# Seven-product stage: the second product ahead of the seventh, and the load of a and b ahead of that of the third block

## The chip, the cores and the metric

The kernel runs on one core of a Trainium2 chip. The metric is the device time of one execution in microseconds (us), lower being better. TensorE does the matrix products, ScalarE and VectorE split numbers and finish the activations, GpSimd and SyncE start transfers from the main memory (GpSimd also those that add to what is already in the on-chip buffer).

## The reference, cut to what matters

```python
# x: 512 tokens x 1024 features; one layer of three sub-layers
def _swiglu(h, w_in, w_out):
    g, u = jnp.split(h @ w_in, 2, axis=-1)      # h 512x1024, w_in 1024x5632
    return (jax.nn.silu(g) * u) @ w_out         # w_out 2816x1024
h = x * (1.0 + scale[:, 2, None, :]) + shift[:, 2, None, :]
y = _swiglu(h, ffn2_w_in[l], ffn2_w_out[l])     # the third sub-layer: here lies the change
x = _layernorm(ALPHA * x + 0.5 * gate[:, 2, None, :] * y, post_ln_g[l, 2], post_ln_b[l, 2])
```

Sub-layers before it are another such feed-forward layer and a mixer (attention and pooling). Everything is float32.

## The kernel before

Every float32 matrix product is made of three passes: each number is split into a rounded high part and the rest, and high times high, high times low and low times high are added up in PSUM. ScalarE makes the high parts (`ACT.Copy` into a rounded type), VectorE the rests (whole minus high), TensorE multiplies.

The first projection of the last feed-forward layer has 22 pairs of tiles: a gate tile and an up tile, each 128 output features by 1024 inputs, for 512 tokens. Pairs 0 to 4 are done plainly. Pairs `T0` = 5 to `FT - 1` = 21 are done by seven half-size products in place of eight, in the manner of Strassen and Winograd: the gate tile is cut into the blocks a and b, the up tile into c and d (each 128 x 512), the tokens into two halves of 256, and the products p1 to p7 use these blocks or their sums. "Block t" below is the work of one such pair. One product is four blocks of inputs by three passes, so 12 matmuls of 128x128 on 256 tokens.

The order of each engine is written out by hand, and semaphores tie them together:

- TensorE, `block_products` (line 1007): for each t p1, p5, p6 of block t, then p4 of block t-1, then p7 and p2 of block t, then p3 of block t-1. p1, p6 and p7 (and p4 later) are accumulated into the same bank, and ScalarE copies the bank's interim values out: `p1_copy` after p1, `u2` after p6, `u3` after p7. So p6 waits for the copy of p1, p7 for the copy `u2`, and p4 (a block later) for the copy `u3`. p2 goes to another bank, and waits for nothing but old sums.
- SyncE, the loop at line 847: in the iteration of t it issues `load_c(t + 2)` (256 KB, after p5 of t), `load_d(t)` (256 KB, after p4 of t-1), `load_a3(t + 2)` (256 KB, after p7 of t) and `load_ab(t + 2)` (512 KB, after p2 of t). A wait at its head holds what is behind it.
- GpSimd, `add_block`: when c of a block has landed, it issues a transfer that adds d to it (line 2574); when the third block (a, loaded by `load_a3`) has landed, one that adds c to it (line 2578). These two sums are the operands of p5 and p7, the tile `raw_13`.
- ScalarE, `block_stage` (line 1596), iteration t: round the two weight blocks of p4 and p3 of t-1 (`hi_d4`, line 1563), the second silu of t-2, copy p1 of t, the first silu of t-1, `a_high` of t-2, round a and b of t+1 (`hi_ab`, line 1540), copy `u2` of t (line 1578), round `raw_2` of t+1 (line 1547), round `raw_13` of t+1 (line 1555), copy `u3` of t (line 1583). The two in the middle matter here: the copy `u2` of a block stands behind the rounding of the next block's a and b.
- VectorE, `block_stage` (line 2204), iteration t: sums of t-2 and t-1, the rest of d4, the weight sums of t+1 (lines 2157 and 2161, which need a, b and the finished c+d), and the rests of ab, 2 and 13 of t+1 (line 2144), the last being the one that p5 of t+1 waits for.

`product_order` (line 93) lists the order of TensorE's products, and all waits on "product so-and-so of block t" are counts derived from that list. After the stage come the units of the second projection (`D2` and on); the first of them land in buffers that the seven products used, so their loads wait for products of the last two blocks.

Of the kernel before, what the change touches and what calls it, by code (L numbers as in the profile page):

```python
# [27 lines left out]
FT = D_FF // P  # L28
# [56 lines left out]
T0 = 5  # L85
D2 = F2 + 2 * T0
# [6 lines left out]
def product_order():  # L93

    out = []
    for t in range(T0, FT + 1):
        if t < FT:
            out += [("p1", t), ("p5", t), ("p6", t)]
        if t > T0:
            out.append(("p4", t - 1))  # L100
        if t < FT:
            out += [("p7", t), ("p2", t)]
        if t > T0:
            out.append(("p3", t - 1))
    return out
# [24 lines left out]
def sum_order():  # L130

    out = [("T", j) for j in range(4)] + [("s2", T0), ("s4", T0)]
    for t in range(T0, FT + 2):
        if t - 2 >= T0:
            out.append(("gb", t - 2))
        if T0 <= t - 1 < FT:
            out.append(("ga", t - 1))
        if t + 1 < FT:
            out += [("s2", t + 1), ("s4", t + 1)]
        if T0 <= t - 1 < FT:  # L140
            out += [("ub", t - 1), ("pa", t - 1)]
    return out
# [18 lines left out]
def counts(order, base):  # L161

    return {step: base + i + 1 for i, step in enumerate(order)}
# [90 lines left out]
def source(n, wunits):  # L254

    half = KD // 2 * P
    if S_FILL <= n < S_A:
        kind, first = FILL[2 * (n - S_FILL)][0], int(FILL[2 * (n - S_FILL)][1])
        if kind == "q":
            return wunits[U_UQ + first // 2]  # L260
        return wunits[U_OUT + first:U_OUT + first + 2, :, half:2 * half].rearrange("t p n -> p t n")
    if S_OUT <= n < F2:
        return wunits[U_OUT + SPLIT_TILES + n - S_OUT]
    if S_A <= n < S_OUT:
        first = 2 * (n - S_A)
        return wunits[U_OUT + first:U_OUT + first + 2, :, 0:half].rearrange("t p n -> p t n")
    return wunits[n if n < D2 else n - D2 + F2_DOWN][:, 0:unit_width(n)]
# [7 lines left out]
def unit_width(n):  # L275

    for down, end in ((F1_DOWN, MX), (D2, STREAM)):
        if down <= n < end and (n - down) % DPM == DPM - 1:
            return LAST_K * P
    return UNIT  # L280


def build(nc, xT, wunits, ada_w, c_rows, pos_rows, cols_dram, pool_w, outT):
# [4 lines left out]
    with ExitStack() as ctx:  # L288
# [84 lines left out]
        def raw_of(n, width):  # L373

            if n == D2:
                return raw_ab[1][:, 0:width]
            if n == D2 + 1:
                return raw_13[1][:, 0:width]
            return raw[:, n % RAWS, 0:width]
# [79 lines left out]
        def in_set(t):  # L459
            return (t - T0) % 2  # L460
# [6 lines left out]
        def raw13(t):  # L467
            return raw_13x if t == T0 + 1 else raw_13[in_set(t)]
# [57 lines left out]
        def pair_banks(t):  # L526
            return (bank[0], bank[1], bank[2]) if t % 2 == 0 else (bank[3], bank[6], bank[7])
# [119 lines left out]
        s_blk, s_bhi, s_blo, s_bsum = s_tp, s_fc, s_tok, s_xk  # L647
        PRODUCT = counts(product_order(), KD)
        ROUNDED = counts(rounding_order(), KD)
        REST = counts(rest_order(), 2 * QB)  # L650
        SUM = counts(sum_order(), QB)
# [68 lines left out]
        def _(sp):  # L720
# [7 lines left out]
            def unit(n):  # L728

                slot, width = n % RAWS, unit_width(n)  # L730
                if D2 <= n < D2 + LEAD + 2:
                    sp.wait_ge(s_blk, PRODUCT[(("p2", FT - 2), ("p2", FT - 2), ("p2", FT - 1), ("p2", FT - 1),
                                               ("p2", FT - 1))[n - D2]])
                    if n >= D2 + RAWS:
                        sp.wait_ge(s_hi, n - RAWS + 1)
                elif n >= RAWS:
                    sp.wait_ge(s_lo, n - RAWS + 1)
                dst = raw_of(n, width)
                if S_FILL <= n < F2 and len(source(n, wunits).shape) == 3:
                    dst = dst.rearrange("p (t n) -> p t n", t=2)  # L740
                sp.dma_start(dst, source(n, wunits)).then_inc(s_raw[slot], 16)
# [15 lines left out]

            unit(0)
            unit(1)
            ada_pair(0)  # L760
            ada_pair(1)
# [35 lines left out]
            def gate_unit(t):  # L797
                return wunits[F2 + 2 * t]
# [4 lines left out]
            def load_c(t):  # L803

                if t == T0:
                    sp.wait_ge(s_lo, D2 - 2)
                elif t == T0 + 1:
                    sp.wait_ge(s_spill, LOADED + 32)
                else:
                    sp.wait_ge(s_blk, PRODUCT["p5", t - 2])  # L810
                sp.dma_start(raw13(t)[:, 0:BLOCK], up_unit(t)[:, 0:BLOCK]).then_inc(s_cl[in_set(t)], 16)

            def load_ab(t):

                if t == T0:
                    sp.wait_ge(s_lo, D2)
                elif t == T0 + 1:
                    sp.wait_ge(s_used, D2 - 1)
                else:
                    sp.wait_ge(s_blk, PRODUCT["p2", t - 2])  # L820
                sp.dma_start(raw_ab[in_set(t)][:], gate_unit(t)).then_inc(s_ab[in_set(t)], 16)

            def load_a3(t):

                if t >= T0 + 2:
                    sp.wait_ge(s_blk, PRODUCT["p7", t - 2])
                sp.dma_start(raw13(t)[:, BLOCK:2 * BLOCK], gate_unit(t)[:, 0:BLOCK])\
                    .then_inc(s_a3[in_set(t)], 16)

            def load_d(t):  # L830

                if t > T0:
                    sp.wait_ge(s_blk, PRODUCT["p4", t - 1])
                sp.dma_start(raw_d4[:, 0, :], up_unit(t)[:, BLOCK:2 * BLOCK]).then_inc(s_d, 16)
# [12 lines left out]
            for t in range(T0, FT - 1):  # L847
                if t + 2 < FT:
                    load_c(t + 2)
                if t > T0:  # L850
                    load_d(t)
                if t + 2 < FT:
                    load_a3(t + 2)
                    load_ab(t + 2)
            unit(D2)
            unit(D2 + 1)
            load_d(FT - 1)
# [26 lines left out]
        def _(pe):  # L884
# [110 lines left out]
            def product(kind, t, out, first, last):  # L995

                hi, lo = block_parts(kind, t)
                for kk in range(KH):
                    cols = slice(kk * P, (kk + 1) * P)
                    high, low = moving(kind, kk)  # L1000
                    nc.tensor.matmul(out[:, 0:HALF], hi[:, cols], high, start=first and kk == 0, stop=False, skip_group_check=True)  # L1001
                    nc.tensor.matmul(out[:, 0:HALF], hi[:, cols], low, start=False, stop=False, skip_group_check=True)  # L1002
                    done = nc.tensor.matmul(out[:, 0:HALF], lo[:, cols], high, start=False, stop=last and kk == KH - 1,  # L1003
                                            skip_group_check=True)
                done.then_inc(s_blk, 1)

            def block_products():

                for t in range(T0, FT):
                    whole, gate_a, mixed = pair_banks(t)  # L1010
                    pe.wait_ge(s_blo, REST["ab", t])
                    if t < T0 + 2:
                        pe.wait_ge(s_prod[1], t - 1)
                    else:
                        pe.wait_ge(s_bsum, SUM["pa", t - 2])
                    product("p1", t, whole, True, True)
                    pe.wait_ge(s_blo, REST["13", t])
                    if t >= T0 + 2:
                        pe.wait_ge(s_bsum, SUM["gb", t - 2])
                    product("p5", t, mixed, True, True)  # L1020
                    pe.wait_ge(s_blo, REST["2", t])
                    pe.wait_ge(s_copy, COPY["p1", t])
                    product("p6", t, whole, False, True)
                    if t > T0:
                        fourth_product(t - 1)
                    pe.wait_ge(s_copy, COPY["u2", t])
                    if t == T0:
                        pe.wait_ge(s_blo, REST["T", 2])
                    product("p7", t, whole, False, True)
                    if t >= T0 + 2:  # L1030
                        pe.wait_ge(s_bsum, SUM["ga", t - 2])
                    product("p2", t, gate_a, True, True)
                    if t > T0:
                        third_product(t - 1)

            def fourth_product(t):

                pe.wait_ge(s_blo, REST["d4", t])
                pe.wait_ge(s_copy, COPY["u3", t])
                product("p4", t, pair_banks(t)[0], False, True)  # L1040
# [201 lines left out]
            for j in range(HEADS // 2):  # L1242
                t = T_KN + j
# [7 lines left out]
            for j in range(QB):  # L1251
                t = T_V + j
# [13 lines left out]
            for hd in range(2):  # L1266
                t = T_Q + hd
# [1486 lines left out]
```

## Time and profile before

| | |
|---|---|
| median of 3 runs | 939.07 us (937.96 to 940.72) |
| profiled execution | 940.3 us, its span 938.5 us |
| TensorE busy in the span | 925.5 us, 99% |
| the stage of seven products | 630.2 us to 801.6 us |
| DMA engines busy in that stage | 69% |

The span is what the profiler saw between the first and the last instruction; the execution's own time has 1.8 us around it. Weight loads (PEld) overlap the matmuls; in this stage one of each starts every 0.12 us, so a pause of TensorE is seen best as the idle time ahead of a weight load. A releaser in square brackets is what ended an idle time; "issue" means that the profile shows no releaser.

### The profile page before, as it was taken

Reading aid. Unit: us, or ns where it says so; the run is one execution under the profiler, and the core shown is the slowest. Engines: PE = TensorE matmul, PEld = TensorE weight load, DVE = VectorE, ACT = ScalarE, POOL = GpSimd, SP = SyncE. Lnnn points to the kernel's source line nnn. Section 1 sums busy time; section 2 is a strip of 40 time slices with the busy share of each in tenths; the row PEclk is TensorE's granted clock in tenths of the full one; section 3 lists DMA queues with packets and bytes.
Section 4 is the critical chain, followed back from the end, with each engine's and each line's share of the span. In section 5 each row is a group of like instructions: output and inputs, shape, how many; then the busy total and the mean of one; then the engine's idle time right before and its main releaser. Section 6 shows DMA issues by size and latency. Waiting matters only on the chain.

```text
span 938.5 us, 12697 instructions
## 1 busy us (share of the span) xinstructions
PE 925.5 (99%) x4845; PEld 778.3 (83%) x4845; DVE 599.6 (64%) x875; ACT 423.3 (45%) x673; POOL 276.7 (29%) x239
## 2 busy tenths in 40 slices
PE   8999999999999999999999999999999999999997
PEld 5788888888888888787776677889999999888886
DVE  6956776545554865687775577787778777433334
ACT  6753223233223132473576656655556565322224
POOL 0021111111113522155863655832111110035124
PEclk9999999999999999999999999999999999999999
DMA  9936566556553663324511112286777775623402
GB/s 359 375 115 213 188 190 200 193 179 206 193 174 129 210 224 122 102 67 135 127 54 46 45 68 69 80 245 169 184 178 180 181 192 143 224 79 107 123 18 89
DMA packets 50507, 144.88 MB, mean 154 GB/s; under 512 B 5264, under 2 KB 7440, under 8 KB 50448
## 3 DMA queue, kind: packets, MB, share of 16 engines
q1 hardware_dynamic: 45008, 134.65, 43.2%
q0 software_dynamic: 4896, 8.92, 6.2%
q8 instruction: 38, 0.62, 0.3%
q10 hardware_dynamic: 544, 0.52, 0.2%
q14 instruction: 21, 0.17, 0.1%
HBM read 138.83 MB, written 4.19 MB: 152 GB/s over the span
## 4 chain that ended last, share of the span: by engine, by line
PE 92%; DMA 5%; DVE 1%; SPq 1%; ACT 1%; issue 0%; ACTq 0%; DVEq 0%
PE bank L890 23%; PE bank L892 23%; PE bank L891 23%; PE bank L1001 5%; PE bank L1003 5%; PE bank L1002 5%; DMA raw<-wunits 4%; PE bank L1304 2%; PE bank L1328 1%; DMA ada_first<-ada_w 1%; PE bank L1315 1%; PE bank L1068 1%; PE bank L975 1%; PE bank L976 1%; PE bank L969 0%
## 5 line engine op out<-in xcount | busy, mean ns | idle before, releaser
L1431 DVE TENSOR_TENSOR w_lo<-raw,w_hi 128x1024 fp32r<-128x1024 f32 (+1 forms) x117 | 160.9, 1385 | 133.2 <-ACT w_hi L1403 132.8
L890 PE MATMUL bank<-h_hi,w_hi 128*128 128x512 f32 x455 | 178.8, 393 | 0.0
L892 PE MATMUL bank<-h_hi,w_lo 128*128 128x512 f32 x455 | 177.2, 389 | 0.0
L891 PE MATMUL bank<-h_lo,w_hi 128*128 128x512 f32 x455 | 177.1, 389 | 0.0
L1403 ACT ACTIVATE w_hi<-raw 128x1024 fp32r<-128x1024 f32 (+1 forms) x118 | 118.8, 1024 | 118.6 <-PE bank L892 111.1
L890 PE MATMUL bank<-a_hi,w_hi 128*128 128x512 f32 (+1 forms) x338 | 128.1, 379 | 0.0
L891 PE MATMUL bank<-a_lo,w_hi 128*128 128x512 f32 (+1 forms) x338 | 127.7, 378 | 0.0
L892 PE MATMUL bank<-a_hi,w_lo 128*128 128x512 f32 (+1 forms) x338 | 127.7, 378 | 0.0
L2539 POOL TENSOR_TENSOR a_lo<-act_t,a_hi 128x512 fp32r<-128x512 f32 x27 | 38.1, 1411 | 251.6 <-ACT a_hi L1526 251.6
L890 PEld LDWEIGHTS bank<-h_hi,w_hi 128*128 128x128 f32 x455 | 85.6, 188 | 17.9 <-issue 0.5
L892 PEld LDWEIGHTS bank<-h_hi,w_lo 128*128 128x128 f32 x455 | 85.4, 188 | 18.0
L891 PEld LDWEIGHTS bank<-h_lo,w_hi 128*128 128x128 f32 x455 | 85.5, 188 | 17.2
L1889 DVE SCALAR_TENSOR_TENSOR var<-ada_ring,c_act 128x1024 bf16<-128x1024 f32 x56 | 72.6, 1296 | 4.1 <-DMA ada_ring<-ada_w 4.1
L890 PEld LDWEIGHTS bank<-a_hi,w_hi 128*128 128x128 f32 x338 | 63.6, 188 | 11.9
L891 PEld LDWEIGHTS bank<-a_lo,w_hi 128*128 128x128 f32 x338 | 63.6, 188 | 11.8
L892 PEld LDWEIGHTS bank<-a_hi,w_lo 128*128 128x128 f32 x338 | 63.6, 188 | 11.8
L1526 ACT ACTIVATE a_hi<-act_t 128x512 fp32r<-128x512 f32 x40 | 25.3, 634 | 78.9 <-DVE act_t L2047 67.7
L1511 ACT ACTIVATE sq<-x 128x512 f32<-128x512 f32 x20 | 12.7, 634 | 105.9 <-DVE x L2035 96.8
L1001 PE MATMUL bank<-t_hi,hi 128*128 128x256 f32 x204 | 58.1, 285 | 2.2 <-ACT u_copy L1578 2.1
L2560 POOL TENSOR_TENSOR s_sum<-s_sum,x 128x512 f32<-128x512 f32 x17 | 27.5, 1616 | 108.0 <-DVE x L2035 105.8
L1002 PE MATMUL bank<-t_lo,hi 128*128 128x256 f32 x204 | 57.7, 283 | 0.0
L1003 PE MATMUL bank<-t_hi,lo 128*128 128x256 f32 x196 | 55.4, 283 | 0.0
(374 smaller groups left out, 1951.4 us busy)
## 6 DMA issues: line engine op xcount, KB each, us to landing
raw<-wunits SPq DMA_DIRECT2D x110, 512.0 KB, 3.5
ada_ring<-ada_w SPq DMA_DIRECT2D x56, 512.0 KB, 4.5
raw_ab<-wunits SPq DMA_DIRECT2D x18, 512.0 KB, 4.7
ada_first<-ada_w SPq DMA_DIRECT2D x16, 512.0 KB, 11.6
raw<-wunits SPq DMA_DIRECT2D x32, 256.0 KB, 3.9
raw<-wunits POOLq DMA_DIRECT2D x32, 256.0 KB, 5.1
raw<-wunits SPq DMA_DIRECT2D x16, 384.0 KB, 3.0
raw_d<-wunits SPq DMA_DIRECT2D x17, 256.0 KB, 2.7
```

What stands on the lines that cost most here:

```text
L890: mm(out, lh, rh, start=first, stop=False)
L891: mm(out, lh, rl, start=False, stop=False)
L892: return mm(out, ll, rh, start=False, stop=last)
L1001: nc.tensor.matmul(out[:, 0:HALF], hi[:, cols], high, start=first and kk == 0, stop=False, skip_group_check=True)
L1002: nc.tensor.matmul(out[:, 0:HALF], hi[:, cols], low, start=False, stop=False, skip_group_check=True)
L1003: done = nc.tensor.matmul(out[:, 0:HALF], lo[:, cols], high, start=False, stop=last and kk == KH - 1, skip_group_check=True)
L1403: nc.scalar.activation(parts(n, 0, width)[0], raw_of(n, width), ACT.Copy)\
L1431: nc.vector.tensor_tensor(lo, raw_of(n, width), hi.bitcast(F32), SUB).then_inc(s_lo, 1)
L1526: fn(a_parts(f, t)[0], act_t[:, t % 2, :], ACT.Copy).then_inc(s_ah[f], 1)
L1889: stt(junk, slot_ap, 1.0, c_act[:], MUL, MUL, accum_out=mod[:, t:t + 1])\
L2539: tt(lo, act_t[:, t % 2, :], hi.bitcast(F32), SUB).then_inc(s_al[f], 1)
L2560: tt(s_sum[:], s_sum[:], x[:, m, :], ADD).then_inc(s_acc[p], 1)
```

## The change

p2 of a block goes ahead of its p7 in TensorE's order (and in the list from which the counts come), with its own wait. In SyncE's order `load_ab(t + 2)` goes ahead of `load_a3(t + 2)`; each keeps its own wait. The loads of the first units after the stage wait for the product that frees their buffer, in the new order.

```diff
@@ product_order
         if t < FT:
-            out += [("p7", t), ("p2", t)]
+            out += [("p2", t), ("p7", t)]
@@ SyncE, unit(n)
                 if D2 <= n < D2 + LEAD + 2:
-                    sp.wait_ge(s_blk, PRODUCT[(("p2", FT - 2), ("p2", FT - 2), ("p2", FT - 1), ("p2", FT - 1),
-                                               ("p2", FT - 1))[n - D2]])
+                    sp.wait_ge(s_blk, PRODUCT[(("p2", FT - 2), ("p7", FT - 2), ("p2", FT - 1), ("p7", FT - 1),
+                                               ("p7", FT - 1))[n - D2]])
@@ SyncE, the loop of the stage
                 if t + 2 < FT:
+                    load_ab(t + 2)
                     load_a3(t + 2)
-                    load_ab(t + 2)
@@ TensorE, block_products
                     if t > T0:
                         fourth_product(t - 1)
+                    if t >= T0 + 2:
+                        pe.wait_ge(s_bsum, SUM["ga", t - 2])
+                    product("p2", t, gate_a, True, True)
                     pe.wait_ge(s_copy, COPY["u2", t])
                     if t == T0:
                         pe.wait_ge(s_blo, REST["T", 2])
                     product("p7", t, whole, False, True)
-                    if t >= T0 + 2:
-                        pe.wait_ge(s_bsum, SUM["ga", t - 2])
-                    product("p2", t, gate_a, True, True)
                     if t > T0:
                         third_product(t - 1)
```

## Rows read from the trace of the kernel before

**Rows 1.** The page: span, TensorE busy, TensorE's granted clock in 40 slices
```profile
span 938.5 us, 12697 instructions
...
PE 925.5 (99%) x4845; PEld 778.3 (83%) x4845; DVE 599.6 (64%) x875; ACT 423.3 (45%) x673; POOL 276.7 (29%) x239
...
PEclk9999999999999999999999999999999999999999
```

**Rows 2.** Stage table (length; busy us per engine; PEclk, DMA share, GB/s)
```profile
630.20:801.60 171.40, 169.22 (x1403) 168.37 (x1402) 131.13 (x195) 96.86 (x164) 27.82 (x31) 1.00 0.69 172
```

**Rows 3.** Timeline of weight loads, the four with idle time ahead (start, length)
```profile
635.35 0.19 PEld L1001 LDWEIGHTS bank<-t_hi,hi 128*128 128x128 f32 x1 [0.68 <-ACT u_copy L1578]
...
644.36 0.19 PEld L1001 LDWEIGHTS bank<-t_hi,hi 128*128 128x128 f32 x1 [0.32 <-ACT u_copy L1578]
...
695.62 0.19 PEld L1001 LDWEIGHTS bank<-t_hi,hi 128*128 128x128 f32 x1 [0.81 <-ACT u_copy L1578]
...
787.56 0.19 PEld L1001 LDWEIGHTS bank<-t_hi,hi 128*128 128x128 f32 x1 [1.18 <-ACT u_copy L1578]
```

**Rows 4.** Timeline of ScalarE ahead of the first, third and fourth pause
```profile
634.92 0.38 ACT L1578 ACTIVATE u_copy<-bank 128x256 f32<-128x256 f32 x1 [1.02 <-PE bank L1003]
...
694.24 1.06 ACT L1540 ACTIVATE hi_ab<-raw_ab 128x1024 fp32r<-128x1024 f32 x1 [1.54 <-DMA raw_ab<-wunits]
695.20 0.36 ACT L1578 ACTIVATE u_copy<-bank 128x256 f32<-128x256 f32 x1
...
786.18 1.06 ACT L1540 ACTIVATE hi_ab<-raw_ab 128x1024 fp32r<-128x1024 f32 x1 [1.91 <-DMA raw_ab<-wunits]
787.15 0.36 ACT L1578 ACTIVATE u_copy<-bank 128x256 f32<-128x256 f32 x1
```

**Rows 5.** Timeline of SyncE's queue over block 17
```profile
753.50 0.33 SPq L811 DMA_DIRECT2D raw<-wunits  x1
756.38 0.33 SPq L834 DMA_DIRECT2D raw_d<-wunits  x1
757.82 0.33 SPq L827 DMA_DIRECT2D raw<-wunits  x1
759.26 0.33 SPq L821 DMA_DIRECT2D raw_ab<-wunits  x1
```

**Rows 6.** Issue to landing, 637 to 792 us: lines 827 (a3), 821 (ab), 2578 (its add)
```profile
DMA to landing us min/median/max: 2.8/4.1/4.7
...
DMA to landing us min/median/max: 4.4/4.7/6.7
...
DMA to landing us min/median/max: 4.0/5.0/6.3
```

**Rows 7.** Landing of the a3 issued at 757.82, and GpSimd's timeline
```profile
DMA to landing us min/median/max: 3.5/3.5/3.5
...
757.66 0.86 POOL L2574 DMA_DIRECT2D raw<-wunits  x1 [5.82 <-DMA raw<-wunits]
761.64 0.86 POOL L2578 DMA_DIRECT2D raw<-wunits  x1 [3.11 <-DMA raw<-wunits]
```

**Rows 8.** ScalarE and VectorE: the latest rounding of raw_13, and its rest
```profile
748.75 1.06 ACT L1555 ACTIVATE hi<-raw 128x1024 fp32r<-128x1024 f32 x1 [2.98 <-issue]
...
749.85 1.22 DVE L2144 TENSOR_TENSOR lo<-raw,hi 128x1024 fp32r<-128x1024 f32 x1 [1.79 <-ACT hi L1555]
```

**Rows 9.** Waits of all engines, 628 to 812 us (total us, times, longest)
```profile
ACT hi L1555 <- issue: 13.8, 11, 3.0
...
ACT hi_ab L1540 <- DMA raw_ab<-wunits: 6.4, 5, 2.3
```

**Rows 10.** Blocks 5 to 7: SyncE's a3 and ab of block 7, GpSimd's add of its a3, its rounding and rest, SyncE's load after p5 of block 7
```profile
637.07 0.33 SPq L827 DMA_DIRECT2D raw<-wunits  x1
638.51 0.33 SPq L821 DMA_DIRECT2D raw_ab<-wunits  x1
...
641.64 0.86 POOL L2578 DMA_DIRECT2D raw<-wunits  x1 [4.36 <-DMA raw<-wunits]
...
646.45 1.06 ACT L1555 ACTIVATE hi<-raw 128x1024 fp32r<-128x1024 f32 x1 [1.62 <-issue]
...
647.54 1.23 DVE L2144 TENSOR_TENSOR lo<-raw,hi 128x1024 fp32r<-128x1024 f32 x1 [0.69 <-ACT hi L1555]
...
651.85 0.33 SPq L811 DMA_DIRECT2D raw<-wunits  x1
```

## The prediction

> **What bounds the kernel now.** I read the page first. TensorE is busy for 99% of the span, at a granted clock that never leaves its upper level, 2.4 GHz [rows 1]. So only time in which TensorE pauses can be won. The table of the stage comes next: 171.40 us, with TensorE busy for 169.22 of them [rows 2]. The reader is to see how little is left: some 2 us by the matmuls, whose ends are modelled. Weight loads show it more sharply. In the timeline of weight loads exactly four of the stage have idle time ahead, 0.68, 0.32, 0.81 and 1.18 us, all released by ScalarE's copy `u2` (line 1578), so all ahead of p7 [rows 3]. A load lasts 0.19 us where the next starts after 0.12, so each pause costs its idle time and 0.07: 0.75, 0.39, 0.88 and 1.25, together 3.27 us. That is all that this stage can give.
>
> ScalarE's timeline tells why the copy is late. In block 5 nothing is in its way: it starts at 634.92, once p6 is done, and TensorE waits out its 0.38 us and the handovers, since block 5 has no p4 of a block before it in between. In the other three the copy stands behind the rounding of the next a and b, which waits for its load: that ends at 695.30 and 787.24 and the copy follows at once [rows 4]. The waits of all engines say that this rounding waited for its load 5 times, 6.4 us in total, and that the rounding of `raw_13` waited 11 times, 13.8 us in total, with no releaser named [rows 9]; what it waits for is the adding transfer of GpSimd.
>
> **The change part by part.** The arithmetic stays: 84 matmuls in a block. One product takes 12 times 0.12 = 1.44 us, as the distance of the two loads behind p7 and p2 shows too, 757.82 to 759.26 [rows 5].
>
> p2 ahead of p7. p7 now starts 1.44 us later after p4 (or p6), and p2 needs no copy. In block 5 the copy is ready 0.75 us after p6's end, less than 1.44. In the latest case, the fourth, it is ready 1.25 us after p4's end, again less than 1.44, even if the load comes no earlier. So all four pauses go: -3.27 us. What is pushed back is small: the copy `u3` waits for p7, now 1.44 us later, but p4 of that block comes only in the middle of the next one, after p3, p1, p5 and p6, 5.8 us on. The sum of p2's result is taken on VectorE in the next block either way: no cost.
>
> ab ahead of a3. Each issue costs SyncE 0.33 us, as before; nothing is added. ab goes out behind p2, which is now where p7 was: 1.44 us earlier. This takes away most of the late roundings (the longest wait was 2.3 us), and of pauses there is nothing left to win. a3 goes out behind p7, 1.44 us later, and now behind 512 KB in the same queue. This is the price. Its chain is: a3 lands, GpSimd issues the add, that lands, ScalarE rounds, VectorE makes the rest, p5 of two blocks later starts. The time for it before: p5 of block 17 starts 1.48 us ahead of the issue behind it, at 752.02; p5 of block 19 is 20.16 us later at 772.18, and the a3 of block 19 goes out at 757.82 [rows 5]. That is 14.36 us; after the change 12.92.
>
> What the chain takes before: 4.1 for a3, 0.3 to 0.35 until GpSimd issues (757.82 and a landing of 3.5, then 761.64 [rows 7]), 5.0 for the add [rows 6], and 2.4 for the rounding and the rest, by the latest of them: 748.75 to 749.85 + 1.22 = 751.07, plus 0.1 of handover [rows 8]. Together 11.85, slack 2.5. That latest one left 0.95 us before p5 at 752.02, which is less than the 1.44 it now loses.
>
> After the change a3 is the second of the pair. Both loads together hold the same bytes and start in the same slot as before, so the second one ends where the second one ended: 4.7 us behind the issue, from 4.4 to 6.7 [rows 6]. The chain is then 4.7 + 0.35 + 5.0 + 2.4 = 12.45, slack 0.5; at best 4.4 + 0.35 + 4.0 + 2.4 = 11.15, slack 1.8; at worst 6.7 + 0.35 + 6.3 + 2.4 = 15.75, late by 2.8. I take the typical value, since the extremes of the two terms were single blocks.
>
> On this the Trainium skill has a rule (DMA: Bandwidth & Descriptors, Queues, rings and completion order): each DMA engine takes the descriptors of one queue in ring order. By it a3 can't overtake the 512 KB ahead. Without it a3 would keep its 4.1 us, the chain 11.85 and the slack 1.1 in place of 0.5. No row of before has a3 behind ab, so this trace doesn't show it.
>
> Block 7 is tighter, as its loads go out while the stage fills. Before, a3 was issued at 637.07, the add at 641.64, and its rest was done at 648.77; p5 started 1.48 ahead of 651.85, at 650.37 [rows 10]. With the two pauses ahead of it gone (1.14 us) p5 wants to start at 649.23. The pair of loads starts 0.75 us earlier and ends, by ab's 638.51 + 4.4, between 642.15 and 642.9; the add goes out 0.35 later, takes its 4.7 again, and then 2.4: 649.6 to 650.4. So p5 waits 0.4 to 1.1 us; I take 0.8. For the other blocks, with a slack of 0.5 and the odd late one, I take 0.4 in all; the ends are 0 and, if the chain stays late, some 8 (below).
>
> The first loads after the stage go out at the same time or 1.44 us earlier; there TensorE doesn't pause before, so nothing is won.
>
> Sum: -3.27 + 0.8 + 0.4 = -2.1 us, 940.3 to 938.2. The 940.3 is the profiled execution; the median, 939.07, is 1.2 us below it. Without any pause in the stage it would be 937.0, and all three timed runs (937.96 to 940.72) lie above that, as they would if the pauses differ from run to run. I read the median as holding about 2 us of pauses, all but some 1.2 of which go. The forecast for the median is thus 938.2 too, -0.9 us or -0.1%.
>
> **The rivals.**
> A, the forecast: pauses ahead of p7 gone, a wait ahead of p5 in block 7 and perhaps one other: 938.2, from 937.4 to 939.8.
> B, no new wait: the add moves from the start of a block to where the loads of c are done, and lands in 4.0 to 4.5 us; slack 1 us. Against it stands block 7's working. 937.0.
> C, slower: p5 waits in most blocks, since a3, second in its queue, and the add behind it, which now runs into the add of c+d, are both slower than typical. It decides from a load and an add of 10.2 us together (12.92 - 0.35 - 2.4), where typical is 9.7 and the worst 13.0. A chain that is late by 0.8 us costs 0.4 a block, as it spans two, in 14 blocks 5.6: 937.0 + 0.8 + 5.6 = 943.4; late by 1.2 it is 946.2. For it speak 11 waits for `raw_13` already [rows 9]; against it, that DMA engines are 69% busy in the stage [rows 2].
> D, the change doesn't do what it says: p7 still waits at its new place, as some other wait ahead of `u2` in ScalarE's order comes last. The pauses stay and block 7's wait comes on top: 940.3. Against it stand the 0.19 us by which even the fourth pause fits under p2, on top of the earlier load.
>
> **How the numbers follow.** Chances: A 0.50, B 0.20, C 0.25, D 0.05. What a measurement of this kernel can tell from no change is about 0.3%, 2.8 us. Faster by that needs B, and a measured before near the profiled 940.3: half of B, 0.10. Slower by that is C but for its mildest part, and a little of D and A: 0.27. Within it, the rest: 0.63. The range is 936.7 to 943.0: below B there is nothing, and it takes in C up to a chain late by 0.7 us; the likeliest case has 937.4 to 939.8 for itself.
>
> **What would show it.** In the timeline of weight loads of the changed kernel the pauses released by `u2` are gone; idle time ahead of p5 (the thirteenth load of a block) behind VectorE's rest (line 2144) shows the price, first in block 7. The load of ab (line 821) is issued 1.44 us ahead of a3 (line 827), a3 takes about 4.7 us to land, and the waits of ScalarE ahead of the rounding of `raw_13` (line 1555) grow from 13.8 us to some 35, as each start is about 2 us later, while those ahead of `hi_ab` shrink. The forecast is wrong if p7 still waits, if a3 lands 5.5 us or more behind its issue, or if p5 waits in more than a few blocks.

## The result: slower by 0.75%, outside the forecast's range

The changed kernel takes 946.24 us (median of 6 runs, 943.56 to 949.12) against 939.16 us before (937.96 to 940.72, 6 runs). The ratio is 1.0075, 95% interval 1.0064 to 1.0086. The forecast was 938.2, with 936.7 to 943.0 as its range: wrong in size and in sign.

The profiled execution has a span of 945.2 us, 6.7 more than before. The page and the stage table answer to [rows 1, 2]: TensorE is busy a little longer by the page, at the same granted clock; the first row of the stage table is 5.8 us longer than before, with about as many recorded matmuls (1397, before 1403).

```profile
span 945.2 us, 12697 instructions
...
PE 927.4 (98%) x4845; PEld 779.2 (82%) x4845; DVE 599.2 (63%) x875; ACT 420.7 (45%) x673; POOL 276.4 (29%) x239
...
PEclk9999999999999999999999999999999999999999
```

```profile
630.40:807.60 177.20, 170.34 (x1397) 168.14 (x1397) 130.28 (x195) 94.48 (x164) 27.77 (x31) 1.00 0.67 166
```

The timeline of weight loads shows the pauses, as in [rows 3]. None is ahead of p7 any more. There are twelve others, 9.84 us together where there were 3.27: the difference, 6.57, is the 6.7 of the spans. Three are ahead of p5 (639.45, 650.60 and 767.40, 1.64 us together; the second is the largest). Nine are ahead of p6, 8.20 us together; the first and the largest of these stand here.

```profile
650.60 0.19 PEld L1001 LDWEIGHTS bank<-t_hi,hi 128*128 128x128 f32 x1 [1.03 <-DVE lo L2144]
...
673.28 0.19 PEld L1001 LDWEIGHTS bank<-t_hi,hi 128*128 128x128 f32 x1 [1.03 <-issue]
...
738.35 0.19 PEld L1001 LDWEIGHTS bank<-t_hi,hi 128*128 128x128 f32 x1 [1.40 <-issue]
```

Which engine held p6 is named by the waits of all engines (total us, times, longest), which answer to [rows 9]: TensorE waited nine times for ScalarE's copy of p1, and ScalarE's rounding of d eight times for its load. Before, neither row was there but for one wait of 1.8 us.

```profile
ACT hi L1555 <- issue: 29.0, 14, 3.5
ACT hi_d L1563 <- DMA raw_d<-wunits: 20.8, 8, 3.3
...
PE bank L1001 <- ACT p_copy L1573: 6.0, 9, 1.2
```

The chain of waits has the whole path of one pause in six lines (pieces under 0.1 us are left out of this view). The load of d, issued at 665.29, takes 6.22 us; behind its rounding stand a silu and the copy of p1 in ScalarE's order; then p6 starts. The 0.94 us put down to "issue" are the rounding, whose row in ScalarE's timeline stands below the chain.

```profile
665.29 6.22 DMA raw_d<-wunits
671.56 0.94 issue
672.50 0.40 ACT act_t L1594
672.89 0.28 ACT p_copy L1573
673.17 0.14 issue
673.31 0.36 PE bank L1001
```

```profile
671.53 1.06 ACT L1563 ACTIVATE hi_d<-raw_d 128x1024 fp32r<-128x1024 f32 x1 [2.48 <-DMA raw_d<-wunits]
```

The timelines of GpSimd and SyncE around that load of d, first of the changed kernel (lines 2578 and 2574 are the adds for the third block and of c+d):

```profile
662.99 0.86 POOL L2578 DMA_DIRECT2D raw<-wunits  x1 [6.56 <-DMA raw<-wunits]
665.29 0.86 POOL L2574 DMA_DIRECT2D raw<-wunits  x1 [1.44 <-DMA raw<-wunits]
...
665.29 0.33 SPq L834 DMA_DIRECT2D raw_d<-wunits  x1
666.73 0.33 SPq L821 DMA_DIRECT2D raw_ab<-wunits  x1
668.17 0.34 SPq L827 DMA_DIRECT2D raw<-wunits  x1
```

then of the same block before, where d (line 834) took 3.4 us:

```profile
659.33 0.86 POOL L2578 DMA_DIRECT2D raw<-wunits  x1 [1.84 <-DMA raw<-wunits]
665.24 0.86 POOL L2574 DMA_DIRECT2D raw<-wunits  x1 [5.04 <-DMA raw<-wunits]
...
664.81 0.33 SPq L834 DMA_DIRECT2D raw_d<-wunits  x1
```

The reader is to see the distance of the two adds: 5.9 us before, 2.3 after; d goes out ahead of the second before, and with it after. Over the stage the median distance is 5.9 us before and 2.0 after. Issue to landing from 637 to 792 us, of lines 811 (c) and 834 (d), before:

```profile
DMA to landing us min/median/max: 2.9/3.8/5.4
...
DMA to landing us min/median/max: 2.6/2.7/5.3
```

and of lines 811 (c), 834 (d), 827 (a3) and 2578 (its add), after:

```profile
DMA to landing us min/median/max: 2.6/2.6/3.5
...
DMA to landing us min/median/max: 2.6/5.8/6.6
...
DMA to landing us min/median/max: 3.9/4.9/6.1
...
DMA to landing us min/median/max: 4.1/4.5/5.2
```

c became faster by 1.2 us, d slower by 3.1. From this came the theory for the experiments: a3 goes out late, so its add does; the load of c then has no add ahead of it and lands sooner (in the block above c goes out at 662.41, 0.6 us ahead of that add, and lands after 2.6); so the c+d add goes out with d, close behind the other add; d is held up, and ScalarE's order hands that on to the copy of p1 and to p6.

### The profile page after: what moved, and what is told of

It reads as the page before. It is cut to its first block, busy times and chain, and to the rows that moved or that the text cites. A ratio compares the mean times of both kernels' runs of the same rounds, so it can differ in the third digit from the quotient of the medians.

```text
span 945.2 us, 12697 instructions
## 1 busy us (share of the span) xinstructions
PE 927.4 (98%) x4845; PEld 779.2 (82%) x4845; DVE 599.2 (63%) x875; ACT 420.7 (45%) x673; POOL 276.4 (29%) x239
## 4 chain that ended last, share of the span: by engine, by line
PE 86%; DMA 8%; issue 2%; DVE 2%; ACT 1%; SPq 1%; ACTq 0%; DVEq 0%
PE bank L890 23%; PE bank L892 23%; PE bank L891 23%; DMA raw_d<-wunits 5%; PE bank L1001 3%; PE bank L1003 3%; PE bank L1002 3%; PE bank L1304 2%; DMA raw<-wunits 2%; PE bank L1328 1%; DMA ada_first<-ada_w 1%; PE bank L1315 1%; PE bank L975 1%; PE bank L969 1%; PE bank L976 1%
```

## The experiments

Times are medians, with the ratio to the kernel before on the same chip. "Slow d" is a load of d of 5 us or more; before has 1 of 16, the changed kernel 10 of 16. Pauses are sums over the stage, read from the timeline of weight loads as above.

**TensorE's order alone.** SyncE's loop has a3 ahead of ab again:

```diff
-                    load_ab(t + 2)
                     load_a3(t + 2)
+                    load_ab(t + 2)
```

> TensorE's new order alone; SyncE keeps a3 ahead of ab. Theory (load of d): in the changed kernel the pauses are ahead of p6, since the load of d takes some 6 us in place of 2.7 when the add of c+d goes out with it or before it. Here a3 still goes out 1.44 us later than in the kernel before, so its add starts later, the load of c lands early and the c+d add meets d: d slow in several blocks, 941 to 946 us. Rival (the third block alone: raw_13 late in its own chain): a3 isn't behind ab here, slack 1.1 us, pauses only in block 7: 938 to 939.5 us.

941.99 us (10 runs), 1.004, interval 1.0025 to 1.0055. Slow d 7 of 16; pauses 4.47 us, none ahead of p7, 0.27 ahead of p5 and 4.20 ahead of p6. a3 lands in 4.4 us here. As the theory has it, and about half of the change's cost comes with this half of it.

**SyncE's order alone.** p7 stays ahead of p2, and ab goes ahead of a3.

> SyncE's new order alone; TensorE keeps p7 ahead of p2, so ab goes out where it did and a3 1.8 us later. Theory (load of d): the c+d add meets d as in the changed kernel, pauses ahead of p6 and p7 both: 945 to 950 us. Rival (the third block alone): pauses ahead of p5 of 0.3 to 1 us in most blocks: 943 to 948 us; the trace tells by the product that pauses.

945.95 us (5 runs), 1.0091, interval 1.0060 to 1.0121. Pauses 10.74 us, of three kinds: ahead of p7 for `u2` (1.53), ahead of p6 (3.92), and ahead of p5 (5.29), most of it four of 0.94 to 1.39 us that end with VectorE's rest of `raw_13`. Slow d 6 of 16. Both the theory and the rival are in it: a3 goes out 9.3 us or more into the block in all blocks after the first, where it was 7.5 in most blocks before and 9.0 at the earliest in the changed kernel, so the third block's own chain is late too.

**The changed kernel, the c+d add held until d has landed.**

```diff
                 if which == 1:
                     pool.wait_ge(s_cl[s], landed(t))
+                    if t >= T0 + 3:
+                        pool.wait_ge(s_d, LOADED + 16 * (t - 2 - T0 + 1))
```

> The changed kernel, with GpSimd's add of c+d held until the load of d of two blocks before it (issued in the same block of TensorE) has landed. Theory (load of d): d lands in 2.6 to 3.1 us in every block, the pauses ahead of p6 go, those ahead of p5 in blocks 6, 7 stay (1.4 us): 938.5 to 941 us. Rival (the third block alone): the a3 chain is as late as before, 945 to 947 us or worse as the adds are nearer to each other.

938.53 us (10 runs), 0.9991, interval 0.9980 to 1.0002. No slow d, none of the pauses ahead of p6; 2.10 us are left, all ahead of p5, 1.29 of it in one block whose a3 took 6.1 us. One wait on GpSimd, which is busy for 29% of the span, takes back the whole loss. Issue to landing of d, 637 to 800 us:

```profile
DMA to landing us min/median/max: 2.6/2.9/4.3
```

**The changed kernel, the copy of p1 ahead of the rounding of d** in ScalarE's order:

```diff
+                    if t < FT:
+                        copied("p1", t)
                     if t > T0:
                         round_block("d4", t - 1)
                     if t >= T0 + 2:
                         silu_second(t - 2)
-                    if t < FT:
-                        copied("p1", t)
```

> The changed kernel, with ScalarE's copy of p1 ahead of its rounding of d in each block. Theory (load of d, through ScalarE's queue): d still lands 5 to 6.5 us after its issue, but p6 no longer waits behind its rounding; what is left is p4's own wait for d, some 0.3 us a block at most, and 1.6 us ahead of p5: 939 to 942 us. Rival (the third block alone): no change, 945 to 947 us, since the copy of p1 isn't what TensorE waits for.

943.03 us (6 runs), 1.0051, interval 1.0032 to 1.0069. No pause ahead of p6 is left, so the copy was what p6 waited for. d is still slow (6 of 16), and now p4 itself waits: 2.46 us in four pauses, 2.22 ahead of p5. I had put the first at 0.3 a block; one was 1.26, where d had taken 7.2 us. The row of that pause, in the timeline of weight loads:

```profile
735.49 0.19 PEld L1001 LDWEIGHTS bank<-t_hi,hi_d 128*128 128x128 f32 x1 [1.19 <-DVE lo_d L2144]
```

**The kernel before, d held until c has landed**, so that d and the c+d add go out together:

```diff
                     sp.wait_ge(s_blk, PRODUCT["p4", t - 1])
+                    if t + 2 < FT:
+                        sp.wait_ge(s_cl[in_set(t)], landed(t + 2))
```

> The kernel before, with the load of d held until the load of c issued ahead of it has landed, which is also what releases GpSimd's add of c+d: so both go out at once, some 0.5 to 2.5 us later than d did. Theory (d is slow whenever the c+d add goes out with it or ahead of it, whatever the orders of a3, ab and of the products): d takes 5 to 7 us in place of 2.7, its rounding waits in most blocks, pauses of 1 to 3 us each ahead of p6: 955 to 975 us. Rival (it is the new place of ab and a3 that slows d): d keeps 2.6 to 3.5 us and lands in time, 939 to 942 us.

940.73 us (9 runs), 1.0027, interval 1.0014 to 1.0039. My theory failed here. The adds went out 0.2 us behind d in most blocks, and d took 2.6 to 2.8 us in 12 of 16. The pauses are 5.13 us, 3.29 of them ahead of p7 as before, so the time is far from the 955 I had expected. One d was slow, 7.3 us: the only one that went out less than 3.6 us after the add for the third block (2.2 us). So the c+d add beside d isn't enough; the other add has to be close ahead as well.

**TensorE's order alone, with the hold.**

> TensorE's new order alone, with GpSimd's add of c+d held until d has landed. Theory: the pauses ahead of p7 (3.3 us in the trace of before, some 2 in its median) and those ahead of p6 are both gone; what stays is one of 0.3 us ahead of p5 and an odd one: 937.2 to 938.5 us, 0.1 to 0.2% faster than before. Rival (the hold costs by delaying the c+d sum): 939 to 941 us.

937.92 us (11 runs), 0.9992, interval 0.9982 to 1.0001. Pauses 0.73 us, all ahead of p5 in blocks 6 and 7.

**The kernel before, with the hold alone.**

> The kernel before with the same hold of the c+d add alone. Theory: d was mostly quick already, so the hold changes little there; the pauses ahead of p7 stay, as they come from u2 and the load of ab: 938.3 to 940 us. Rival (the hold is itself what makes the version with both orders as fast as before, and has nothing to do with the change): 937 to 938 us.

937.87 us (11 runs), 0.9993, interval 0.9984 to 1.0002. The rival's number. The pauses ahead of p7 in blocks 5 and 6 stay (1.15 us), but the two later ones are gone: they came of a late load of ab, and in this trace ab takes 4.3 to 5.2 us where it took up to 6.7. So what the new order of products was to win, holding one add gives as well, and neither order is then better: 937.92 and 937.87. None of the three versions with the hold is shown faster than before, as each interval takes in 1.

**A tiny load ahead of d in the changed kernel.**

```diff
+                    if t > T0 + 1:
+                        sp.wait_ge(s_x[7], 16 + 16 * (t - T0 - 1))
+                    sp.dma_start(page[:], cols_dram[:, 0:16]).then_inc(s_x[7], 16)
                 sp.dma_start(raw_d4[:, 0, :], up_unit(t)[:, BLOCK:2 * BLOCK]).then_inc(s_d, 16)
```

> The changed kernel with a load of 64 bytes a partition, 8 KB in all, issued just ahead of each load of d, into a tile that nobody reads. It asks what holds d. If the bytes of d wait for their share of the DMA engines beside the add, the tiny one lands in some 2 us while d takes 6. If a transfer's completion is held until the add's earlier writes have landed, the tiny one takes 5 to 6 us too, and lands with d and the add. Time 946 to 952 us, as d goes out 0.4 us later.

943.74 us (1 run, so without an interval), less than expected. The 8 KB take 4.1 us in the median, 2.0 to 5.4, beside d's 5.1. Issue to landing from 637 to 800 us, of the tiny load and of d:

```profile
DMA to landing us min/median/max: 2.0/4.1/5.4
...
DMA to landing us min/median/max: 3.4/5.1/6.6
```

In the block at 739 us the tiny one, issued at 739.11, landed after 5.1 us; d, issued at 739.48, after 5.1; the c+d add, issued at 738.54, after 5.5: all three between 744.0 and 744.6. So it isn't the number of bytes of d. The Trainium skill (DMA: Bandwidth & Descriptors, Queues, rings and completion order) has a rule by which a transfer's signal lands only after every earlier write of the same DMA engine, across its queues; that block agrees.

So do all twelve traces. SyncE's loads were issued 163 times 0.6 to 2.0 us behind an add still under way, and landed after it each time; 43 times less than 0.25 us behind one, and landed ahead of it each time. The tiny load of 2.0 us is of the second kind (0.1 us behind a c+d add), and the d issued 0.4 us behind it took 5.1. Starting an add takes GpSimd 0.86 us, so an add just started may have no write ahead of the load's yet; that is my reading, and no run here tests it. In the changed kernel five of the ten slow d went out 0.8 to 1.4 us behind the c+d add and landed 0.2 us after it. Four more went out within 0.3 us of it and landed 0.2 us ahead of it, after some 6 us, which that order alone doesn't explain. What holds these, and whether d waits in the queue or only its signal does, stays open.

**The kernel before, the add for the third block held until p5 is done**, the sufficient cause alone:

```diff
                     pool.wait_ge(s_a3[s], landed(t))
+                    if t >= T0 + 2:
+                        pool.wait_ge(s_blk, PRODUCT["p5", t - 1])
```

> The kernel before with one edit: GpSimd's add for the third block of t+1 is held until p5 of t is done, so it goes out some 1.5 us later, as in the changed kernel; no product and no load is moved. Theory, as the runs so far have shaped it: d is slow when it goes out between two adds close to each other (that of the third block less than some 3.2 us ahead, that of c+d with it). Then c, with no add beside it, lands in 2.6 to 3 us, its add goes out with d, d takes 5 to 6.5 us in most blocks, and pauses stand ahead of p6: 942 to 947 us. Rival (the places of ab, a3 or p2 are needed for it): d keeps 2.6 to 3.5 us, 938 to 940 us.

944.27 us (4 runs), 1.006, interval 1.0043 to 1.0077. No load and no product is moved, and the loss is there: c lands in 2.6 to 3.3 us (median 2.7), slow d 9 of 16, pauses 9.73 us, of which 8.20 ahead of p6. The add goes out 3.8 us into the block in the median, where it was 1.8 before and 4.2 in the changed kernel. Issue to landing from 637 to 800 us, of c and of d:

```profile
DMA to landing us min/median/max: 2.6/2.7/3.3
...
DMA to landing us min/median/max: 3.4/5.5/6.6
```

Its waits show the same pair of rows as the changed kernel's:

```profile
ACT hi_d L1563 <- DMA raw_d<-wunits: 24.1, 10, 3.7
...
PE bank L1001 <- ACT p_copy L1573: 6.1, 6, 1.2
```

**The same with the hold of the c+d add.**

> The run before it plus the hold of the c+d add until d has landed. Theory: d back at 2.6 to 3.5 us, no pauses ahead of p6: 937.5 to 939.5 us. Rival (the later add of the third block costs by itself, through raw_13): as late as without the hold.

938.79 us (10 runs), 1.0005, interval 0.9996 to 1.0015. Slow d 0 of 16, pauses 1.25 us. So the later add of the third block shows no cost by itself; it costs through the c+d add and d.

## Why the prediction was wrong, by its steps

- *All four pauses ahead of p7 go.* Right: none is left, -3.27 us.
- *The copy `u3` and the sum of p2 cost nothing.* Right, no row shows them.
- *a3 lands 4.7 us behind its issue, its add takes 5.0.* 4.9 and 4.5, together 9.4 for a forecast 9.7. The slack was there: in the changed kernel with the hold, p5 waits in three blocks only.
- *p5 waits 0.4 to 1.1 us in block 7; I take 0.8, and 0.4 elsewhere.* 1.10, and 0.54 in two others: 1.64 for a forecast 1.2. I had read the start of p5 off the issue of the load behind it and so put every deadline some 0.3 us too late: by the weight loads, p5 of block 17 starts at 751.75, not 752.02.
- *"Each issue costs SyncE 0.33 us, as before; nothing is added"*, and no price for the loads of c and d. This is the step that failed. I followed a3 and ab down their own chain, and left out whom the moved add meets. The forecast had -2.1 us of pauses, the trace has +6.57; of the 8.64 between them 8.20 are this step's, and 0.44 the pauses ahead of p5. The trace of before had the sign: its one slow d, 5.3 us, went out 2.6 us after the add for the third block (at 641.64, [rows 10]) and 0.3 us before the c+d add. It was in block 6, and I took it for the filling of the stage. The load of d and the c+d add, from the timelines of before:

```profile
644.27 0.33 SPq L834 DMA_DIRECT2D raw_d<-wunits  x1
...
644.55 0.86 POOL L2574 DMA_DIRECT2D raw<-wunits  x1 [2.05 <-DMA raw<-wunits]
```

- Rival C had the sum (943.4 to 946.2), with the wrong place: I put it ahead of p5, where 1.64 us stand, and for another reason. The order within one queue that I weighed there is borne out: in all 15 blocks a3 landed behind the ab issued ahead of it, by 0.6 us in 14. With a3 ahead of ab (TensorE's order alone) it took 4.4 us and not 4.9, and 4.20 us of pauses stood ahead of p6 and not 8.20. So the place behind ab adds to the loss, but as far as the runs tell only by making the add later: with the c+d add held, the same places of a3 and ab show no loss (938.53 us).
- *The signs of being wrong.* None of the three came: p7 doesn't wait, a3 takes 4.9 us in the median (the sign was 5.5), p5 waits in three blocks. The waits ahead of the rounding of `raw_13` grew about as forecast (29.0 and 3.8 us, for a forecast 35). My list looked only at the chain that I had followed, and the loss stood outside it.
- *The median holds about 2 us of pauses.* Right, as far as it can be told: the spans of the profiled versions but the tiny load's, less their pauses, are 934.8 to 936.0 us (five within 0.2 of 935.2), so with 1.8 us around the span 936.6 to 937.8 is left without any pause, and the median before, 939.16, holds 1.4 to 2.6.

## What to carry to other kernels

When a transfer is moved, list what else is in flight at its new place, and what its absence speeds up at the old one: the load that paid here was moved by nobody. A load that becomes faster can hurt, when its landing releases a transfer that then meets another. And where an in-order engine has a wait for a load ahead of a short copy, the copy's reader pays for every late load.

## What the hardware showed that I had not expected

- The load of d, 256 KB, took 2.6 to 3.4 us in 15 of 16 blocks of the kernel before, and 5 to 7.3 us in the blocks in which it went out between two adding transfers close to each other. Over before, the changed kernel, TensorE's order alone and d held until c has landed, 18 of the 19 loads of d of 5 us or more went out at most 3.1 us behind the one add and at most 0.3 us ahead of the other; the last was 3.2 us behind. The other versions widen that place: of the nine such loads with the add for the third block held, four went out 0.4 to 0.5 us ahead of the c+d add. Over all twelve traces the 48 slow loads of d went out at most 3.2 us behind the one add and at most 0.6 us ahead of the other, or behind it. In that place 20 others took 2.6 to 4.9 us; of the 124 elsewhere none took more than 4.6. So the place is needed, and doesn't settle the length.
- 36 of the 48 slow loads of d landed within 0.2 us of the c+d add, ahead of it or after it.
- An 8 KB load just ahead of d took 3.3 us or more in 14 of 15 cases. Nine of the 15 went out in the narrower of the two places above (at most 3.2 us behind the one add, 0.3 ahead of the other); eight of these took 3.5 to 5.4 us.
- With one adding transfer held by some 2 us and nothing else changed, the longest load of ab took 5.2 us and not 6.7. This is one trace of each, and the median of ab stayed at 4.7 to 4.8.
